# An expert unit's last SwiGLU block: its subtraction ahead of weight splits, its turning inside the down step in front

## The reference

```python
def swiglu(h, w_gu, w_down):
    g, u = jnp.split(h @ w_gu, 2, axis=-1)
    return (jax.nn.silu(g) * u) @ w_down

def moe_swiglu(h, w_router, w_gu, w_down):
    ...
    top_logit, top_e = lax.top_k(logits, TOP_K)
    gates = jax.nn.softmax(top_logit, axis=-1).astype(h.dtype)
    ...
    def expert_block(args):
        xb, e = args
        return swiglu(xb, w_gu[e], w_down[e])
    ...
```

## Time and profile before

| | |
|---|---|
| median of 3 runs | 2803.29 us (2800.68 to 2804.34) |
| the profiled execution | 2802.33 us, span 2800.4 us |
| PE busy | 2542.1 us, 91% |
| DVE, ACT busy | 1708.0 us (61%), 1254.2 us (45%) |
| mean granted clock of TensorE | 0.946 |
| expert stage, from the first rows turned to the last matmul | about 1446 to 2691 us |

### The profile page before, as it was taken

How to read it: one execution, slowest core, us unless ns; L and a number is a source line. 1 busy time by engine, 2 the same in 40 slices (tenths; PEclk the granted TensorE clock), 3 DMA queues, 4 the chain that set the end, 5 groups by cost and what they waited for, 6 DMA issues and landing times.

```text
span 2800.4 us, 31443 instructions
## 1 busy us (share of the span) xinstructions
PE 2542.1 (91%) x12526; PEld 2038.5 (73%) x12526; DVE 1708.0 (61%) x2010; ACT 1254.2 (45%) x1400; POOL 240.6 (9%) x240
## 2 busy tenths in 40 slices
PE   4988898889999997788869999999999999999977
PEld 2444564468887885787769988898889977998853
DVE  5697797432323223494347678666877678667852
ACT  2343343032222222355225567565765667556741
POOL 3012844100000000000000000000000000000010
PEclk9999989999999998669969999999999999999989
DMA  7445610122322231535057689877987699777950
GB/s 233 143 142 170 168 61 31 38 83 90 106 90 90 91 105 61 117 135 188 11 195 247 236 316 371 274 244 248 379 307 258 238 331 369 241 258 248 374 198 30
DMA packets 316338, 526.14 MB, mean 188 GB/s; under 512 B 19238, under 2 KB 175498, under 8 KB 313530
## 3 DMA queue, kind: packets, MB, share of 16 engines
q1 hardware_dynamic: 287114, 479.73, 50.1%
q0 software_dynamic: 5888, 25.78, 2.9%
q10 hardware_dynamic: 23184, 18.55, 2.1%
HBM read 494.46 MB, written 45.81 MB: 193 GB/s over the span
## 4 chain that ended last, share of the span: by engine, by line
PE 79%; DVE 10%; ACT 4%; POOL 3%; issue 2%; DMA 2%; ACTq 0%; DVEq 0%; POOLq 0%; SPq 0%
PE psum L1762 25%; PE psum L1350 16%; PE psum L1821 11%; PE psum L1608 6%; PE psum L1823 4%; PE psum L1245 4%; PE psum L1268 2%; PE psum L1679 2%; DVE stages_r L3175 1%; PE psum L1699 1%; ACT stages_r L2297 1%; PE psum L1419 1%; POOL stages L1071 1%; POOL stages L1074 1%; PE psum L1696 1%
## 5 line engine op out<-in xcount | busy, mean ns | idle before, releaser
L3175 DVE TENSOR_TENSOR stages_r<-kept,stages_r 128x2048 fp32r<-128x2048 f32 x336 | 769.2, 2291 | 271.2 <-ACT stages_r L2297 270.3
L1762 PE MATMUL psum<-stages_r 128*128 128x512 f32 x3136 | 746.3, 396 | 21.0 <-DVE stages_r L3230 11.1
L2297 ACT ACTIVATE stages_r<-kept 128x2048 fp32r<-128x2048 f32 x336 | 637.3, 1912 | 263.4 <-PE psum L1762 136.6
L1762 PEld LDWEIGHTS psum<-stages_r 128*128 128x128 f32 x3136 | 589.2, 190 | 148.1 <-DVE stages_r L3175 12.4
L1821 PE MATMUL psum<-stages_r 128*128 128x320 f32 x1792 | 465.8, 346 | 6.3 <-issue 3.2
L1350 PE MATMUL psum<-stages_r 128*128 128x512 f32 x1920 | 440.0, 392 | 11.5 <-DVE stages_r L2857 11.5
L1350 PEld LDWEIGHTS psum<-stages_r 128*128 128x128 f32 x1920 | 363.0, 189 | 87.7 <-issue 11.9
L1823 PE MATMUL psum<-stages_r 128*128 128x160 f32 x1792 | 423.6, 236 | 0.0
L2857 DVE TENSOR_TENSOR stages_r<-kept,stages_r 128x2048 fp32r<-128x2048 f32 x54 | 123.6, 2293 | 365.6 <-ACT stages_r L2157 365.6
L1823 PEld LDWEIGHTS psum<-stages_r 128*128 128x128 f32 x1792 | 343.4, 192 | 2.0
L1821 PEld LDWEIGHTS psum<-stages_r 128*128 128x128 f32 x1792 | 337.7, 188 | 9.0 <-DVE stages_r L3175 3.8
(11 more groups left out here) (399 smaller groups left out, 2513.5 us busy)
## 6 DMA issues: line engine op xcount, KB each, us to landing
kept<-in_moe_w_gu_dram SPq DMA_DIRECT2D x224, 1024.0 KB, 6.1
kept<-in_moe_w_down_dram SPq DMA_DIRECT2D x112, 1024.0 KB, 5.8
kept<-in_ffn_w_gu_dram SPq DMA_DIRECT2D x28, 1024.0 KB, 5.1
kept<-in_ev_w_in_dram SPq DMA_DIRECT2D x16, 1024.0 KB, 7.3
kept<-in_ffn_w_down_dram SPq DMA_DIRECT2D x14, 1024.0 KB, 5.0
s_output_maps_by_state<-stages ACTq DMA_DIRECT2D x64, 128.0 KB, 2.0
s_input_maps<-stages ACTq DMA_DIRECT2D x32, 256.0 KB, 2.5
s_output_maps<-s_output_maps_by_state SPq DMA_DIRECT2D x32, 256.0 KB, 4.7
```

Of the source, the lines that this page charges most:

```text
L1762: m = pe.matmul(out_, a, b, start=start and n == 0, stop=stop and n == len(pairs) - 1, skip_group_check=True)
L2297: act.activation(w_high[n % WSLOTS], unit_tile(n), ACT.Copy).then_inc(s_wh, 1)
L3175: dve.tensor_tensor(w_low[n % WSLOTS], unit_tile(n), w_high[n % WSLOTS], ALU.subtract).then_inc(s_ws, 1)
```

## The change

At a **large** unit's end (step 13), VectorE's two subtractions L3215 and L3216 stand in front of the split of tile n + 4 (which is the next unit's tile 0), no longer behind it. At a **small** unit's end, down(5) is cut in its two sides (12 matmuls each). TensorE now makes: up(6), first side of down(5), `turn_hidden(6)`, `turn_rows(i + 1)`, second side of down(5), down(6). ScalarE and VectorE put `hidden_high(6)` / `hidden_low(6)` in front of the split of tile 41, and the rows between the splits of tile 41 and of the next unit's tile 0. No instruction is added or removed, and the order of the splits stays.

```diff
-                def down(s_):
+                def down(s_, sides=(0, 1)):
...
-                    for side in range(2):
+                    for side in sides:
...
                     rows_by(2 + s_ % 2, [sup_at(s_, kk) for kk in range(2)])
-                    if s_:
+                    if 0 < s_ < SSTEPS - 1:
                         down(s_ - 1)
+                down(SSTEPS - 2, (0,))
                 turn_hidden(SSTEPS - 1)
                 if chained:
                     turn_rows(i + 1)
+                down(SSTEPS - 2, (1,))
                 down(SSTEPS - 1)
...
-                    if s_:
+                    if 0 < s_ < SSTEPS - 1:
                         for side in range(2):
                             split(i, sdown_at(s_ - 1, side) + WSLOTS)
                 hidden_high(SSTEPS - 1)
+                split(i, sdown_at(SSTEPS - 2, 0) + WSLOTS)
                 if chained:
                     rows_high(i + 1)
+                split(i, sdown_at(SSTEPS - 2, 1) + WSLOTS)
...
                     m.then_inc(s_hid, 1)
-                    split(i, n + 1 + WSLOTS)
+                    if s_ < STEPS - 1:
+                        split(i, n + 1 + WSLOTS)
                     dve.wait_ge(s_hdA, hidden_base(i) + s_ + 1)
                     hd = hid_l[s_ % 2]
                     dve.tensor_tensor(hd[:, :, 2 * P:3 * P], lhid[:, :, 0:P], hd[:, :, 0:P], ALU.subtract)
                     dve.tensor_tensor(hd[:, :, CAP:CAP + REST], lhid[:, :, P:CAP], hd[:, :, P:CAP], ALU.subtract).then_inc(s_hdr, 1)
+                    if s_ == STEPS - 1:
+                        split(i, n + 1 + WSLOTS)
                     if s_:
                         split(i, down_at(s_ - 1) + WSLOTS)
...
-                    if s_:
+                    if 0 < s_ < SSTEPS - 1:
                         for side in range(2):
                             split(i, sdown_at(s_ - 1, side) + WSLOTS)
                 hidden_low(SSTEPS - 1)
+                split(i, sdown_at(SSTEPS - 2, 0) + WSLOTS)
                 if chained:
                     rows_low(i + 1)
+                split(i, sdown_at(SSTEPS - 2, 1) + WSLOTS)
```

## The result

| | before | changed |
|---|---|---|
| median of 4 runs | 2803.82 us (2800.68 to 2805.31) | 2774.82 us (2771.60 to 2777.85) |
| ratio, 95% interval | | 0.9898 (0.9881 to 0.9915) |
| profiled execution, span | 2800.4 us | 2773.1 us |
| expert stage, from the first rows turned (L1770) to the end of the last L1762 | 1446.6 to 2690.8: 1244.1 us | 1445.7 to 2663.2: 1217.5 us |
| behind it | 109.6 us | 109.9 us |

The kernel is 1.02% faster. Of the 27.3 us between the two spans 26.7 lie in the expert stage; 0.9 us is a start of that stage that was earlier by chance (no code ahead of it changed), and 0.3 us went the other way behind it.

A forecast was written before the change was run, and what follows sets the result against it. TensorE's idle time at eight unit ends and slow matmuls behind it were the bound. Large ends 12.9 plus small ends 13.9 made 26.8 us off 2802.33: 2775.5, adjusted to 2776.0; own range 2772 to 2780, to 2785 with (a) and (b).

The forecast's parts named there:

- Large ends, stop of 2.50 us gone and 0.75 new: Four large unit ends: subtractions ahead of the split replace each 2.50 us stop by 0.75 us; 12.9 us won in all.
- The 0.25 us within the first step: Behind a large end: a 0.25 us wait for a split, covered by the next unit starting 0.75 us late.
- Small ends, margins: Four small unit ends: subtraction done at 2.3 us margin, next unit asking at 1760.0, stops gone; 13.9 us won.
- The smallest margin: At small ends, the block's product is ready 0.37 us before TensorE turns the block, so no wait.
- The clock: Behind unit-end stops TensorE's clock fell to 0.50 in five cases, making matmuls slow by 7.8 us in all.
- (a): Rival at unit ends: stops go but the clock falls as often as now; 7.8 us less won, 2784, chance 0.12.
- (b): Rival: only small ends keep slow stretches, as transposes don't hold the clock; 4.3 us less, 2780, chance 0.12.
- (c): Rival: small ends give nothing, the turning waits for the product; 13.9 us lost, 2789, chance 0.08.
- (d): Rival in small units: weight transfers become the bound and the units stay as long; 2789, chance 0.04.
- (e): Rival at unit ends: the next unit's start stays where it is, nothing moves; 2802, chance 0.03.
- (f): Rival: cut down steps thin TensorE's work at unit ends and the clock stays at 0.50; slower, 2808, chance 0.03.
- The tail: Behind unit 7, the last store overlaps more with the last gate weights; loss between nothing and 1.8 us, taken as 0.

The follow-up runs named there:

- filled_stops: The kernel before, with TensorE's eight stops at unit ends filled with transposes of a constant of the same length; 0.9973 of before, expert stage 1236.5 us.
- rows_first: The changed kernel, with VectorE making the rows' low half ahead of the second split at large ends; 0.9886 of the kernel before, expert stage 1214.2 us.
- more_transposes: The changed kernel, with the eight row transposes at the three small ends that turn rows made five times; 2783.57 us in one execution.
- turn_first: The changed kernel, with the last block at small ends turned ahead of both halves of down(5), not between them; 2790.49 us in one execution.
- late_gate: The changed kernel, with SP issuing the last 4 MB of gate weights only after four of eight gathers have landed; 0.9890 of the kernel before.
- the parts alone: The two runs with one edit each, large_only and small_only; 0.9964 and 0.9944 of the kernel before.
- small_only: The changed kernel with the large units' edit undone, so the small units' part alone; 0.9944 of the kernel before, expert stage 1226.6 us.
- large_only: The kernel before with the large units' edit alone, the two subtractions ahead of the split; 0.9964 of before, expert stage 1233.7 us.
- the one with three more edits: The changed kernel with rows_first, late_gate and a large unit's first gate-and-up sum ahead of a split; 2768.08 us, on repeat 2767.74 us.

## Why the prediction was right

The forecast was 2776.0 us with a range of 2772 to 2785; measured were 2774.82 and 2775.67. By its own steps:

- **What bounds the kernel**: TensorE's idle time at unit ends and the slow matmuls behind it. Confirmed by taking the one without the other (`filled_stops`).
- **Large ends, stop of 2.50 us gone and 0.75 new**: the new one is 0.84 at unit 0 and 0.80 at the others. That it is the rows' low half behind a second split is shown by `rows_first`. I looked for it on L3185; the profile put it down to "issue", naming no engine, and only the row of L3189, which ends at 1636.50 where the matmuls start at 1636.60, and the experiment settle it. The 0.25 us within the first step was covered by that stop and came back without it.
- **Small ends, margins**: set on the time scale of before (2.65 us later at this place, by the forecast turning at 1749.57 against 1746.92), the subtraction ended at 1751.97 (forecast 1752.1) and the next unit started at 1759.9 (1760.0). The smallest margin held: forecast 0.37, measured 0.40.
- **The clock**: all five slow stretches went, 7.8 us by the rows, 7.6 by `filled_stops`. Rivals (a) and (b) fall. For (b) the transposes had to let the clock fall, and 5.5 us of them did not. The Trainium skill (TensorE: Matmul & The Clock Gate, Part 4: PE-mode transpose) says that transposes don't count as keeping TensorE busy; for the float32 transposes of this kernel `more_transposes` shows the opposite, a granted clock of 1.00 over 5.5 us of them. Whether they would also raise a clock that stands at 0.50, no run here shows.
- **Rival (c)** fell with the margin, and `turn_first` shows what a wait at the turning costs, 18.0 us in one execution, 4 more than I gave (c), with slow stretches in it. **(d)** fell: unit 1's stretch moved 373 GB/s where it had moved 362, and ScalarE waited for no transfer. **(e)** and **(f)** fell. In (f) the saving without the clock's share, 18.4 us, doesn't follow from the terms of the sum: 9.99 + 11.06 - 3.0 are 18.05, and 19.1 with a wait of 0.26 covered at each large end. That changes nothing else in the forecast.
- **The tail**, bounded by 0 and 1.8 us and taken as 0: 0.3 us. The store took 0.75 us longer than before (8.64 against 7.89 us in the earlier trace rows) and part of that came back behind it. `late_gate` shows the whole of the term that lay there unused: with the weights out of its way the store needs 4.07 us.
- **The sum**: 26.8 us forecast, 26.7 us in the expert stage. That it meets to 0.1 us is in part luck: the large ends gave 12.5 instead of 12.9 (the new stops are 0.24 us longer in all than the 0.75 each; 0.2 are left unexplained) and the small ones 14.35 instead of 13.9 (0.25 of it at unit 7, with the cause open), and the two misses cancel. The medians' 29.0 and 26.4 us lie around it, as the part ahead of the stage moves by more than these differences.

What the forecast had too simple is the count of five slow stretches. It was read from one execution and went into the sum as if it held in each; the parts alone show by how much that can be off, 1.9 us one way and 3.2 the other at ends whose stops were unchanged.

## What to carry to other kernels

Where an engine's list mixes work for now (the last block's subtraction) with work ahead (the next tile's split), read at each end of a loop which of the two stands in front, and count the idle time that a wait in the wrong one makes together with what comes behind it: here 21.1 us of idle time drew another 7.8 us of slow matmuls. Before a stop is taken out, write down what is late next and by how much; here that gave 0.75 us at one kind of end and nothing at the other. A single profile's slow stretches should be kept as a term of their own with a range, not folded into the stops.

## What the runs showed of the hardware

- Whether TensorE's clock falls to 0.50 behind a stop differs between stops of one length. Within the stages profiled: behind stops of 0.8 us never; behind 1.84 us in neither of two; behind 2.22 us at three of four (`turn_first`); behind 2.50 us at three of four (before) and one of four (`small_only`); behind 3.07 or 3.08 us at two of three (before) and three of three (`large_only`). A fall cost 1.4 to 1.65 us in nine cases in these three kernels and at unit 7 in `turn_first`; at units 1 and 3 in `turn_first`, where the slow stretch lasted over 6 us, it cost 2.9 and 3.1.
- Float32 transposes on TensorE keep its clock at 1.00, both as filling of 2.5 to 3.1 us (`filled_stops`) and for 5.5 us on end (`more_transposes`). They did not prevent a fall behind a stop: at unit 3's end in `turn_first` the eight of L1770 right behind the 2.22 us took 1.87 us, where they take 1.04 at full clock.
- The expert stage repeats closely (1217.45 and 1217.26 us for the changed kernel, 1212.1 and 1212.2 for the one with three more edits), while its start lies between 1442 and 1451 us in the profiled executions, with the same code ahead of it. The two profiled executions of the changed kernel are 4.2 us apart in span and 4.7 in the start of the stage. So the 6 to 8 us by which its executions spread come, as far as these two show, from the part ahead, and differences of 2 us are to be read within the stage.
